# Weight columns per matmul doubled to 512 in the q, k and V products of a two-layer kernel, with first loads and sums of squares in pieces

## What is computed

```python
h = rms_norm(x, g)                       # layer A
qkv = h @ w_qkv                          # 1024 x 3072
q = rope(rms_norm(q, g_q), pos)          # per head of 64
k = rope(rms_norm(k, g_k), pos)
o = diff_attention(q, k_all, v_all, lam, pos0)
o = rms_norm(o, g_sub) * (1.0 - lam_init)    # per head of 128
...
kv = rms_norm(x, kv_norm_g) @ w_kv_s     # layer B: k and v, 1024 columns each
```

## Time and profile before

| what | value |
|---|---|
| median of 3 runs | 1700.36 us (1698.76 to 1701.44) |
| the profiled execution's own time | 1698.16 us |
| its span | 1696.5 us |
| granted clock, mean | 0.999 |
| TensorE busy | 1660.5 us, 98% |
| VectorE busy | 1146.6 us, 68% |
| ScalarE busy | 750.5 us, 44% |
| GpSimd busy | 160.5 us, 9% |
| chain that ended last | TensorE 85%, VectorE 9%, ScalarE 3%, issue 2% |
| DMA | 266.48 MB, mean 157 GB/s |

### The profile page before, as it was taken

How to read it: one execution, slowest core, us unless ns; L and a number is a source line. 1 busy time by engine, 2 the same in 40 slices (tenths; PEclk the granted TensorE clock), 3 DMA queues, 4 the chain that set the end, 5 groups by cost and what they waited for, 6 DMA issues and landing times.

```text
span 1696.5 us, 33302 instructions
## 1 busy us (share of the span) xinstructions
PE 1660.5 (98%) x14036; PEld 1529.8 (90%) x14036; DVE 1146.6 (68%) x1587; ACT 750.5 (44%) x1269; POOL 160.5 (9%) x155
## 2 busy tenths in 40 slices
PE   7999999999999999999999999999999999999999
PEld 7999766679999999999999995566799999999999
DVE  7654266667994698488742326888679946974884
ACT  5443266665552254135432215667555423441441
POOL 0000000003210012011000000000031100110120
PEclk9999999999999999999999999999999999999999
DMA  6235699941222122212243258998312221222222
GB/s 255 72 105 180 243 409 409 409 184 50 84 91 100 51 100 77 99 50 100 100 162 137 103 209 330 407 393 325 138 51 100 87 96 67 75 100 75 75 100 88
DMA packets 40047, 266.48 MB, mean 157 GB/s; under 512 B 4704, under 2 KB 5216, under 8 KB 10720
## 3 DMA queue, kind: packets, MB, share of 16 engines
q1 hardware_dynamic: 36144, 252.88, 39.3%
q0 software_dynamic: 3760, 11.54, 2.0%
HBM read 247.63 MB, written 15.73 MB: 155 GB/s over the span
## 4 chain that ended last, share of the span: by engine, by line
PE 85%; DVE 9%; ACT 3%; issue 2%; DMA 0%; SPq 0%; DVEq 0%; ACTq 0%
PE ps L568 29%; PE ps L790 26%; PE ps L267 5%; PE ps L269 5%; PE ps L268 5%; PE ps L1207 3%; DVE s_lo L739 3%; PE ps L1158 2%; PE ps L1186 2%; PE ps L604 2%; PE ps L1173 2%; PE ps L1261 1%; DVE rows L1575 1%; PE ps L1231 1%; PE ps L1243 1%
## 5 line engine op out<-in xcount | busy, mean ns | idle before, releaser
L267 PE MATMUL ps<-w_hi,h_hi 128*128 128x256 f32 x640 | 183.0, 286 | 9.9 <-DVE h_lo L299 9.9
L268 PE MATMUL ps<-w_lo,h_hi 128*128 128x256 f32 x640 | 181.9, 284 | 0.0
L269 PE MATMUL ps<-w_hi,h_lo 128*128 128x256 f32 x640 | 181.9, 284 | 0.0
L245 DVE TENSOR_TENSOR w_lo<-w_raw,w_hi 128x2048 fp32r<-128x2048 f32 x55 | 126.0, 2291 | 79.3 <-ACT w_hi L229 79.3
L735 ACT ACTIVATE s_hi<-t 128x512 fp32r<-128x512 f32 x176 | 109.5, 627 | 152.0 <-PE ps L790 70.7
L229 ACT ACTIVATE w_hi<-w_raw 128x2048 fp32r<-128x2048 f32 x54 | 103.1, 1910 | 166.3 <-PE ps L568 158.7
L790 PE MATMUL ps<-hs_hi,s_hi 128*128 128x320 f32 x528 | 163.8, 310 | 2.2 <-DVE s_lo L739 2.2
L790 PE MATMUL ps<-hs_hi,s_lo 128*128 128x320 f32 x528 | 163.2, 309 | 0.0
L790 PE MATMUL ps<-hs_lo,s_hi 128*128 128x320 f32 x528 | 163.2, 309 | 0.0
L568 PE MATMUL ps<-gu_hi,w_hi 128*128 128x320 f32 x692 | 157.8, 309 | 0.2
L568 PE MATMUL ps<-gu_lo,w_hi 128*128 128x320 f32 x692 | 157.7, 309 | 0.0
(11 more groups left out here) (262 smaller groups left out, 4109.3 us busy)
## 6 DMA issues: line engine op xcount, KB each, us to landing
w_raw<-in_w SPq DMA_DIRECT2D x99, 1024.0 KB, 4.8
kv<-in_k_a SPq DMA_DIRECT2D x12, 1024.0 KB, 9.7
kv<-in_v_a SPq DMA_DIRECT2D x12, 1024.0 KB, 9.4
kv<-in_v_s SPq DMA_DIRECT2D x12, 1024.0 KB, 8.1
kv<-in_k_s SPq DMA_DIRECT2D x12, 1024.0 KB, 9.3
xT<-in_k_a SPq DMA_DIRECT2D x8, 1024.0 KB, 9.8
xT<-in_k_s SPq DMA_DIRECT2D x8, 1024.0 KB, 9.3
work<-in_v_a SPq DMA_DIRECT2D x7, 1024.0 KB, 9.8
```

The costliest lines, as they stand in the source:

```text
L245: nc.vector.tensor_tensor(w_lo[s][:, :, :], w_raw[:, s, :, :], w_hi[s][:, :, :].bitcast(F32), ALU.subtract).then_inc(lo_done, 1)
L267: nc.tensor.matmul(out, s_hi, m_hi, start=first, stop=False, skip_group_check=True)
L268: nc.tensor.matmul(out, s_hi, m_lo, start=False, stop=False, skip_group_check=True)
L269: return nc.tensor.matmul(out, s_lo, m_hi, start=False, stop=last, skip_group_check=True)
```

## The change

A unit of w_qkv and of the V half of w_kv_s is now four k tiles by 512 columns, still 1 MB and 128 x 2048 (`wide_units_of`; `wide` views the buffers so). Two units make one group of 512 columns: even units hold k tiles 0 to 3, odd ones 4 to 7, and the PSUM bank is accumulated over both. `token_evac` evicts 512 columns after the odd unit. The q and k of a pair are squared, normed and rotated as two halves one after the other, with the weight splits between; `sqs` is gone and the square goes to `swp`. The loops on the engines are written out. GpSimd's stores of v wait for the double groups: quarters 0 and 1 for the first, 2 and 3 for the second.

First loads: four pieces of 256 KB of unit 0 in turn with four single x tiles, `small` behind the first two, then x tiles in two pairs and unit 1. The split of unit 1 moves ahead of the squares and their sum; the 10 small matmuls stand after the second token tile of unit 1. VectorE splits unit 2 behind the rotation tables and lambda.

Sums of squares in attention A, for the seven heads inside the loop: the square (moved to the next pair, behind `act_w1`) is copied to fp32r `sub_hi` on ScalarE, behind `act_osb`; VectorE makes `sub_lo`, behind `dve_w2` and ahead of `dve_pm`; TensorE runs two fp32r matmuls with `ones_r` where the f32 one was. In layer B four of the eight `h_lo` tiles may be rewritten once unit 2 of V is done. Some semaphores are merged.

```diff
...
+            sb(s, "pad_sub", [P, 4096 + KT * TOK + 4 * KT * UC + 4 * SEQ + SEQ + 4])
+            sub_hi = sb(s, "sub_hi", [P, SEQ], F32R)
+            sb(s, "pad_sub2", [P, SEQ + 8])
+            sub_lo = sb(s, "sub_lo", [P, SEQ], F32R)
...
+        def wide(x):
+
+            return x[:, :, :].rearrange("p k c -> p (k c)").rearrange("p (k c) -> p k c", k=KT // 2)
+
+        def token_product(t, s, i):
+
+            k = s * KT // 2 + i
+            tokens = slice(t * P, (t + 1) * P)
+            return mm3(ps[:, t, :], h_hi[:, k, tokens], h_lo[:, k, tokens], wide(w_hi[s])[:, i, :],
+                       wide(w_lo[s])[:, i, :], k == 0, k == KT - 1)
+
+        def first_unit(pe, h_ready):
+
+            for i in range(KT // 2):
+                pe.wait_ge(*((piece["lo"], i + 1) if i < 3 else (lo_done, 1)))
+                pe.wait_ge(h_ready[0], i + 1)
+                for t in range(TT):
+                    last = token_product(t, 0, i)
+                    if i == KT // 2 - 1:
+                        last.then_inc(mm, 1)
+
+        def token_unit(pe, ph, j, ev, free=None, k_done=None, between=None):
+
+            pe.wait_ge(lo_done, split_count(ph, j))
             for t in range(TT):
-                if ev0 is not None:
-                    pe.wait_ge(ev, j * TT + (ev0 + t - TT + 1))
-                elif free is not None:
+                if j % 2 == 0 and j > 0:
+                    pe.wait_ge(ev, (j // 2 - 1) * TT + t + 1)
+                elif j == 0 and free is not None:
                     free(t)
-                for k in range(KT):
-                    last = product(t, k)
-                    if k_done is not None and t == TT - 1 and k < KT - 1:
+                for i in range(KT // 2):
+                    last = token_product(t, j % 2, i)
+                    if k_done is not None and t == TT - 1 and i < KT // 2 - 1:
                         last.then_inc(k_done, 1)
                 last.then_inc(mm, 1)
-
-        def token_evac(act, ph, j, dst, ev):
+                if between is not None:
+                    between(t)
+
+        def token_evac(act, ph, m, dst, ev):
             for t in range(TT):
-                act.wait_ge(mm, tiles_before(ph, j) + (t + 1))
-                nc.scalar.activation(dst(t), ps[:, t, 0:UC], ACT.Copy, scale=rstd_col[:, t:t + 1]).then_inc(ev, 1)
+                act.wait_ge(mm, tiles_before(ph, 2 * m + 1) + (t + 1))
+                nc.scalar.activation(dst(t), ps[:, t, :], ACT.Copy, scale=rstd_col[:, t:t + 1]).then_inc(ev, 1)
...
+        stage = work[:, 0:4, :].rearrange("p a n -> p (a n)").rearrange("p (t c) -> p t c", t=TT)
+        rot, swp = quarter(2), quarter(3)
...
+        def qk_square(act, j):
+            act.wait_ge(qk["ev"], (j // 2 + 1) * TT)
+            if j > 0:
                 act.wait_ge(qk["rot"], j)
-            token_evac(act, "qkv", j, lambda t: stage[:, t, :], qk["ev"])
-            act.wait_ge(qk["ev"], j * TT + TT)
-            nc.scalar.activation(sqs, stage, ACT.Square).then_inc(qk["sq"], 1)
+            nc.scalar.activation(swp, half_stage(j), ACT.Square).then_inc(qk["sq"], 1)
+
+        def qk_root(act, j):
...
+        def qk_dve(dve, ch, j):
+            which, part = j // 4, half_stage(j)
...
+                    if n % 2 == 0 and n > 0:
+                        self.sub_sq(n // 2 - 1)
                     if n > 0:
                         self.act_osb(n - 1)
+                    if n % 2 == 0 and n > 0:
+                        self.sub_high(n // 2 - 1)
...
-                        if n + 1 < N_PAIRS:
-                            self.sub_sq(n // 2)
...
+                    if n % 2 == 0 and n > 0:
+                        self.sub_low(n // 2 - 1)
...
+            def sub_high(self, r):
+                act, s = nc.scalar, self.s
+                act.wait_ge(s["sq"], r + 1)
+                nc.scalar.activation(sub_hi[:, :], self.sub_buf(r)[:, 0, :], ACT.Copy).then_inc(s["sh"], 1)
+
+            def sub_low(self, r):
+                s = self.s
+                nc.vector.wait_ge(s["sh"], r + 1)
+                nc.vector.tensor_tensor(sub_lo[:, :], self.sub_buf(r)[:, 0, :], sub_hi[:, :].bitcast(F32),
+                                        ALU.subtract).then_inc(s["sl"], 1)
+
             def sub_pe(self, r):
                 pe, s = nc.tensor, self.s
+                if r < 7:
+                    pe.wait_ge(s["sl"], r + 1)
+                    pe.wait_ge(s["wne"], 2 * r + 3)
+                    nc.tensor.matmul(self.sub_ps(r), ones_r[:, :], sub_hi[:, :], start=True, stop=False)
+                    nc.tensor.matmul(self.sub_ps(r), ones_r[:, :], sub_lo[:, :], start=False, stop=True)\
+                        .then_inc(s["ms"], 1)
+                    return
                 pe.wait_ge(s["sq"], r + 1)
-                if r < 7:
-                    pe.wait_ge(s["wne"], 2 * r + 3)
                 nc.tensor.matmul(self.sub_ps(r), ones[:, :], self.sub_buf(r)[:, 0, :], start=True, stop=True)\
...
-            half = KT // 2 * UC
-            sp_.dma_start(w_raw[:, 0, 0:KT // 2, :].rearrange("p k c -> p (k c)"), a_w[0, :, 0:half])\
-                .then_inc(loaded["head"], 16)
-            load_x(0)
-            sp_.dma_start(w_raw[:, 0, KT // 2:KT, :].rearrange("p k c -> p (k c)"), a_w[0, :, half:2 * half])\
-                .then_inc(loaded["raw0"], 16)
-            for i in range(1, 4):
-                load_x(i)
+            def load_x(tiles, name):
+                sp_.dma_start(xT[:, tiles, :], a_x[:, tiles, :]).then_inc(loaded[name], 16)
+
+            for i in range(4):
+                sp_.dma_start(w_raw[:, 0, 2 * i:2 * i + 2, :].rearrange("p k c -> p (k c)"),
+                              a_w[0, :, 2 * i * UC:(2 * i + 2) * UC])\
+                    .then_inc(loaded[f"w{i}" if i < 3 else "raw0"], 16)
+                load_x(slice(i, i + 1), ("tile0", "x0", "tile2", "x1")[i])
+                if i == 0:
+                    sp_.dma_start(small[:, :], a_small).then_inc(loaded["small"], 16)
+            load_x(slice(4, 6), "x2")
+            load_x(slice(6, 8), "x3")
...
-                pool.wait_ge(qk["ev"], (9 + j) * TT)
+                pool.wait_ge(qk["ev"], (5 + j // 2) * TT)
...
+            first_hi(act, 0)
             act.wait_ge(setup["small"], 1)
+            x_tile = [(loaded[n], 16) for n in ("tile0", "x0", "tile2", "x1", "x2", "x2", "x3", "x3")]
             for i in range(4):
-                first_hi(act, i)
-                for t in range(2 * i, 2 * i + 2):
-                    first.hi(act, t, (loaded[f"x{i}"], 16))
+                if i > 0:
+                    first_hi(act, i)
+                first.hi(act, i, x_tile[i])
+            for t in range(4, KT):
+                first.hi(act, t, x_tile[t])
+            split_hi(act, "qkv", 1, 1)
             for t in range(KT):
-                first.square(act, t, (loaded[f"x{t // 2}"], 16))
-            split_hi(act, "qkv", 1, 1)
+                first.square(act, t, x_tile[t])
             act.wait_ge(loaded["masks"], 16)
             nc.scalar.activation(steps[:, :], v5[:, 0, 0:M_S], ACT.Copy)
+            nc.scalar.activation(ones_r[:, :], ones[:, :], ACT.Copy)
             nc.scalar.activation(new_mask[:, :], v5[:, 0, M_S:M_N], ACT.Copy).then_inc(setup["const"], 1)
+            split_hi(act, "qkv", 2, 0)
             first.root(act, 5)
-            act.wait_ge(setup["lam_in"], 1)
-            nc.scalar.activation(st[:, 4:6], st[:, 4:6], ACT.Exp).then_inc(setup["lam_exp"], 1)
-            act.wait_ge(norm["cols"], 1)
-
-            qk_act(act, 0, 0)
-            with act.Fori(0, 3) as i:
-                for k in (1, 2):
-                    qk_act(act, i * 2 + k, k % 2)
-                    qk_tevac(act, i * 2 + (k - 1))
-            qk_act(act, 7, 1)
-            qk_tevac(act, 6)
-            for j in range(8, 12):
-                if j < 11:
-                    split_hi(act, "qkv", j + 1, 1 - j % 2)
-                token_evac(act, "qkv", j, lambda t: v5[:, t, (j - 8) * UC:(j - 7) * UC], qk["ev"])
-                if j == 8:
-                    qk_tevac(act, 7)
-            ta.act_a(act, [(qk["ev"], 12 * TT), (qk["stored"], 64)], "oa", [(qk["vstored"], 64)])
+            act.wait_ge(setup["lam"], 1)
+            nc.scalar.activation(st[:, 4:6], st[:, 4:6], ACT.Exp).then_inc(setup["lam"], 1)
+            act.wait_ge(norm["cols"], 2)
+
+            token_evac(act, "qkv", 0, lambda t: stage[:, t, :], qk["ev"])
+            for m in range(1, 5):
+                a, b = 2 * m - 2, 2 * m - 1
+                qk_square(act, a)
+                qk_root(act, a)
+                split_hi(act, "qkv", 2 * m + 1, 1)
+                qk_square(act, b)
+                qk_root(act, b)
+                split_hi(act, "qkv", 2 * m + 2, 0)
+                qk_tevac(act, a)
+                if m < 4:
+                    act.wait_ge(qk["rot"], b + 1)
+                    token_evac(act, "qkv", m, lambda t: stage[:, t, :], qk["ev"])
+                else:
```

(26 more changed lines are left out.)

170 lines of the change are left out of this document (51 added, 119 removed).

## The result

| | before | after |
|---|---|---|
| median | 1700.02 us, 4 runs (1698.76 to 1701.44) | 1685.3 us, 4 runs (1684.34 to 1686.59) |
| ratio | | 0.9915 (0.9903 to 0.9927) |
| profiled execution, its span | 1698.16, 1696.5 us | 1685.07, 1683.3 us |

The change gives 14.7 us.

A forecast was written before the change was run, and what follows sets the result against it. TensorE was taken as busy nearly throughout, so edits count by shortening its queue or making it wait. From 1698.16 us, -9.6 - 3.2 + 0.15 - 1.4 + 4.1 - 1.0 = -10.95 gave 1687.2 profiled, 1689.4 median; range 1687 to 1691.5, 8 in 10 1683.5 to 1695.5.

The forecast's parts named there:

- Part 1: Projection and layer-B V product: 512-column matmuls take 226.7 ns, against 240 for two of 256; gains 9.6 and 3.2 us.
- (c): 512-column matmuls: the fixed part grows with the columns, 240 ns each, 12.8 us missing, 1702.2 us; chance 0.04.
- (d): Matmuls of both products: 512 columns don't stream at one column per cycle, slower, up to 1956 us; chance 0.03.
- Part 2: q/k chain in the projection: weight splits come in time, over 3 us slack; wider last eviction at the seam +0.15 us.
- Part 3: First loads: smaller pieces let TensorE start at 8.5 instead of 9.86 us; gain 1.4 us, bounds 0 and 2.7.
- Part 4: Seam before attention A: a second v store delays vnew by 9 us against 4.9 margin; stall 4.1 us, bounds 0 and 6.1.
- rival (b): Seam: the vnew wait is longer, or TensorE's clock falls in it; 1693.2 us, at most 1697.7; chance 0.13.
- signs named for being wrong: Matmul spacing over 230 ns, the two stores drained by 212, or a unit's split coming late.
- rival (a): Seam: the second store isn't in the way and no vnew wait appears; 1685.3 us; chance 0.27.
- Part 5: Attention A sums of squares: moved square frees 0.45 us, subtraction pushes 0.3 back; 0.15 us per pair of rounds, 1.0 over seven.

The follow-up runs named there:

- mm_256: Kernel after, with each 512-column matmul of the two products issued as two of 256 columns; 1698.12 us, ratio 0.9985 to the kernel before.
- stores_last: Kernel after, with the last two stores of v issued behind the two memsets and first two vnew loads on GpSimd's queue; 1684.98 us, ratio 0.9905.
- two_stores: Kernel before, with the store of v quarter 2 held until quarter 3 is evicted too; 1701.42 us, ratio 1.0002.
- four_stores: Kernel after, with all four stores of layer A's V held back until its last eviction; 1693.17 us, ratio 0.9963.
- zeros_on_act: Kernel after, with the zeroings of swn and vnew in layer A's attention done by ScalarE, not GpSimd; 1683.1 us, ratio 0.9902.
- zeros_f32: Kernel after, with those zeroings on ScalarE and the sums of squares by one f32 matmul at the new place; 1682.51 us, ratio 0.9896.
- sub_f32_moved: Kernel after, with the square at its new place but the plain f32 matmul, no copy or subtraction; 1685.48 us, ratio 0.9915.
- mm_128: Kernel after, with each 512-column matmul of the two products issued as four of 128 columns; 1994.11 us, 1 run.

## Why the prediction was right, and where it was not

**Part 1 holds to the tenth.** 227 ns per matmul, as the line through 256 and 320 columns gave it. (The texts on record call the two levels 2.4 and 1.2 GHz. No trace gives a frequency: 2.4 is 1 over the 0.417 ns per column, and 1.2 is the 256 columns over the 213 ns of the earlier trace rows, each if a column takes one cycle, which is my estimate. That 0.417 ns is the full rate, on which the choice of 12.8 us leaned, was shown by no row; the 227 ns show that it holds up to 512 columns.) From its first matmul to the first of q the V product takes 54.43 instead of 57.59 us. `mm_256` takes the gain away again, 12.0 to 12.8 us at the same clock. Rivals (c) and (d) fall with it.

**Part 2 holds**: no wait for a split in 175.5 us. The wider last eviction took 0.69 us (I had 0.60 to 0.63), which put TensorE's restart 0.22 us later, not 0.15.

**Part 3**: `small` landed at 6.01 (forecast 6.25) and TensorE started at 8.19 (8.5), so 1.67 us where I had 1.4. Some of the earlier start is worked at the lower clock: in the traces of nine kernels with 512 columns the level rises between 11.4 and 14.0 us, not at a fixed distance from the first matmul, and the projection's last matmul starts between 182.8 and 184.0 with it where the new loads lead.

**Part 4 is the step that failed, by the size of a term.** I took 9 us for a second store ahead of `vnew`, from the 11 us that one contended store takes to land. That was the time of one store from issue to landing, and stores under way overlap in it: the second store of the kernel after, issued 0.88 us behind the first, landed 5.0 us behind it (196.1 and 201.1). The first `vnew` landed 5.8 us after its issue with no late store ahead (`stores_last`), 9.1 with one, 12.3 and 12.7 with two (`two_stores` and the kernel after) and 20.3 with four, so a store adds 3.2 to 3.8 us. Against a margin of 4.9 us one more gives no wait. It lay inside my bounds (1.9 to 11) near the lower one, where the row of the uncontended store, 3.9 us, was the better guide; the "some 2 us that overlap" stood on no row. `four_stores` shows that the wait itself was rightly seen: it comes where the margin is used up, and the clock falls in it, as in rival (b). Of the signs named for being wrong, one came: both stores had drained (by 201.1 us) before `vnew` was wanted.
That a second store too would land before `vnew` stood on one row, `vnew` 0.9 us behind the single store. The traces bear it out: it landed 0.3 us behind the last of two stores in the kernel after, 0.2 in `two_stores`, and 0.7 behind the last of four.

**The number is partly luck.** The sum without the wait is 1685.3, and so is the median, to the tenth. But with the terms as measured (parts 1, 2, 3 and 5, and the memset) it is -9.6 - 3.2 + 0.22 - 1.67 - 2.0 + 0.86 = -15.4 us for the -15.05 of rival (a), with errors of both signs, and the difference of the kernels reads 14.7 us in the medians, 13.1 in the two profiled runs and 15.5 to 15.9 at the same clock.

**What part 4 left out.** Moving the store by 0.87 us moved what is behind it on GpSimd, and I costed only the DMAs. The memset of `vnew` now meets VectorE's scale: 0.86 us at the seam. `two_stores` makes it without the rest of the change, `stores_last` moves it to `sel`, `zeros_on_act` removes it. Behind it TensorE's clock falls for some 3 us, another 0.6 us in the profiled run. That fall isn't tied to the delay: in `mm_256` the delay is there and the clock doesn't fall (1.00 from 180 to 212), in `zeros_on_act` and `zeros_f32` the delay is gone and it falls for longer. The profiled run of the kernel before, in which it didn't fall here, has a mean clock of 0.999, as only 4 of 35 other runs of that kernel have. So it may fall there too in others, and what decides it isn't shown.

**Part 5**: the period fell by 0.32 us, not 0.15. The mechanism was as forecast, with one term mis-sized: the square out of the way of the exponential gives the 0.45 us, and the two pieces, for which I had a push of 0.3, cost 0.13. So the split that the part was made for brings nothing, and the place of the square brings it all. Whether the 0.13 is the push through `dve_pm` isn't shown. Over attention A the 0.3 us per two pairs give 2.0 us in the profiled run, and 0.86 + 0.6 go back, so the stage's end moved by 0.5 us only, where I had 1.0 less the wait. The undoing costs 3.8 us by the medians, but 1.8 to 2.6 us at the same clock, which fits the 2 us of periods.

**What stays open.** From 353.7 to the first feed-forward matmul the kernel after loses 0.33 us (13.30 for 12.96 us); it waits 0.99 us for VectorE where before it waited 0.64. Why VectorE starts late isn't shown. In attention B the kernel after loses 1.1 us at 1016 to 1024, where its clock reads 0.50 and 0.66; in the kernel before it reads 0.65 and 0.92 in the stretch that answers to it. What sets how long it falls, there and behind the seam, wasn't found. `sub_f32_moved` gained 0.13 us per period over the kernel after and nothing by the median; in its trace the second pair of the attention starts 1.35 us later (207.07 for 205.72), with the clock down for some 7 us behind the seam.

## What to carry to other kernels

A fixed cost per matmul can be read from two widths of one trace (13.3 ns here), and merging matmuls saved it in both stages where TensorE is full (12.0 to 12.8 us together, at the same clock). A transfer's time to landing (11.0 us for the store here) is no price for what is queued behind it: take what one more transfer adds (3.2 to 3.8 us). A difference of 1 to 3 us between two kernels of this length says little until the mean clocks of the runs are set side by side, and one profile per kernel doesn't show what makes the clock fall. When an instruction moves on an engine's queue, list everything behind it, memsets too, and ask what each will now run beside on the other engines.

## What the runs showed of the hardware

- Starts of fp32r matmuls, each with its own weight load, lay 120 ns apart at 256 columns (the kernel before, `mm_256`), 146.7 ns at 320 (the kernel before) and 226.7 ns at 512 (the kernel after). These three are columns x 0.417 ns + 13.3 ns. At 128 columns it was 111 ns (`mm_128`), which isn't.
- At the start of every trace starts lay farther apart for a time: 213 ns at 256 columns (9.86 to 13.84 us, the kernel before) and 426 ns at 512 (8.19 to 12.16, the kernel after). With 128 columns it was 213 ns for 211 us, without a wait in them (`mm_128`).
- Behind the seam the clock stayed at 1.00 with TensorE idle for 1.37, 0.95 and 0.74 us (`mm_256`), fell to 0.66 and 0.91 in two windows of 4 us with the same idle times (the kernel after), and to 0.88, 0.50 and 0.76 or 0.77 in three with 0.51, 0.95 and 0.69 us (`zeros_on_act`, `zeros_f32`).
- A store of 640 KB ahead on GpSimd's queue, with the DMA share at 1.01 to 1.02, added 3.2 us (`two_stores`) to 3.8 us (`four_stores`) to the landing of a load of 32 KB, while such a store itself took 10.1 us (`mm_256`) to 22.3 us (`four_stores`) from issue to landing.
- A `TENSOR_SCALAR` of VectorE beside a memset of GpSimd took 1.21 us (the kernel after), 1.22 (`two_stores`) and 0.92 (`stores_last`), and each ended within 0.1 us of the memset's end; with no memset beside them the first two took 0.35 us (`zeros_on_act`) and the last 0.26 us (the kernel after). One that began 0.26 us before the end of a memset took its usual 0.35 us (the kernel before). Beside the issue of stores one took 1.15 us (`four_stores`) and another its usual 0.26 (`two_stores`). A `TENSOR_REDUCE` from PSUM over 1040 columns took 1.23 us beside the memsets in `four_stores` and 1.23 us without them (`zeros_on_act`); one of 256 columns right behind the long operation of `stores_last` took 0.62 us for 0.42. How a memset makes the one kind longer isn't shown.
- Runs of one kernel differ by 2 to 3 us with the mean clock: 1701.2, 1699.9 and 1698.5 us at 0.997, 0.998 and 0.999 for the kernel before.
